# A decoder block with product-key experts: the gate of the one-hot masks moves from VectorE to ACT, and dot rows move from one stage to the next

## What is computed

```python
q = (h @ w_q).reshape(T, 8, 256)
s1 = einsum('thd,kd->thk', q[..., :128], k1)     # 128 keys each
s2 = einsum('thd,kd->thk', q[..., 128:], k2)
v1, i1 = top_k(s1, 16);  v2, i2 = top_k(s2, 16)
top, pos = top_k(all 256 sums of v1 and v2, 16)
idx = i1 * 128 + i2 at pos;  g = softmax(top)    # 8 heads x 16 experts a token
act = gelu(einsum('thkd,td->thk', u_tab[idx], h)) * g
out = einsum('thk,thkd->td', act, v_tab[idx])    # 16384 experts of width 2048
```

## Time and profile before

| | |
|---|---|
| median of 3 runs | 1833.39 us (1832.21 to 1834.75) |
| profiled execution | 1831.69 us |
| its span | 1829.7 us |
| TensorE busy | 1792.3 us, 98% |
| VectorE busy | 1586.5 us, 87% |
| ACT busy | 824.2 us, 45% |
| mean granted TensorE clock | 0.998 |
| HBM traffic | 337 GB/s over the span |

### The profile page before, as it was taken

One profiled execution on the slowest core, in us unless ns is written; L12 is line 12 of the kernel. 1 busy time (PEld: TensorE's weight loads), 2 busy tenths in 40 slices (PEclk: granted clock), 3 DMA queues, 4 the chain that ended last, 5 costly groups with the idle time before them and its releaser, 6 DMA issues.

```text
span 1829.7 us, 29108 instructions
## 1 busy us (share of the span) xinstructions
PE 1792.3 (98%) x9962; PEld 1571.9 (86%) x9962; DVE 1586.5 (87%) x2605; ACT 824.2 (45%) x1187; POOL 207.4 (11%) x193
## 2 busy tenths in 40 slices
PE   6999999999999999999999999999999999999998
PEld 6878888445999999999999999997888888888886
DVE  4668899966778999999999999998888888888887
ACT  3011222302635554333566666664555555555544
POOL 1000000110000000110122111121111111111110
PEclk9999999999999999999999999999999999999999
DMA  9998766798686667988899999999999999999994
GB/s 385 420 422 339 278 253 252 283 422 356 253 323 247 239 240 251 376 330 329 333 347 371 362 357 363 364 359 378 385 366 370 365 369 372 366 370 365 371 372 206
DMA packets 98193, 617.98 MB, mean 338 GB/s; under 512 B 13233, under 2 KB 21969, under 8 KB 26449
## 3 DMA queue, kind: packets, MB, share of 16 engines
q1 hardware_dynamic: 61456, 415.26, 59.0%
q0 software_dynamic: 25408, 184.58, 26.5%
q10 hardware_dynamic: 11266, 17.32, 2.5%
HBM read 600.26 MB, written 16.79 MB: 337 GB/s over the span
## 4 chain that ended last, share of the span: by engine, by line
PE 77%; DVE 10%; DMA 9%; issue 3%; ACT 1%; SPq 0%; DVEq 0%; ACTq 0%
PE ps L1320 30%; PE ps L960 15%; PE ps L967 9%; DMA raw<-in_w_ada 6%; PE ps L1005 6%; PE ps L1121 5%; PE ps L1175 4%; PE ps L1272 2%; PE ps L1016 2%; DVE big L1402 2%; DVE raw L1427 1%; DVE w_low L1380 1%; DMA big<-in_w_gate_f 1%; DVE big L1483 1%; DMA raw<-in_peer_v 1%
## 5 line engine op out<-in xcount | busy, mean ns | idle before, releaser
L673 ACT ACTIVATE w_hi<-raw 128x1024 fp32r<-128x1024 f32 x520 | 551.0, 1060 | 492.6 <-PE ps L1320 239.4
L1380 DVE TENSOR_TENSOR w_low<-raw,w_hi 128x1024 fp32r<-128x1024 f32 x520 | 632.9, 1223 | 89.6 <-ACT w_hi L673 82.8
L1320 PE MATMUL ps<-w_hi,a 128*128 128x512 f32 x1536 | 390.2, 389 | 0.5 <-issue 0.3
L960 PE MATMUL ps<-a,w_hi 128*128 128x384 f32 x1856 | 374.2, 343 | 0.9 <-issue 0.8
L1320 PEld LDWEIGHTS ps<-w_hi,a 128*128 128x128 f32 x1536 | 288.3, 188 | 60.9 <-ACT w_hi L673 0.5
L960 PEld LDWEIGHTS ps<-a,w_hi 128*128 128x128 f32 x1856 | 316.0, 189 | 1.9 <-issue 1.7
L1320 PE MATMUL ps<-w_low,a 128*128 128x512 f32 x1024 | 274.3, 390 | 1.2 <-DVE w_low L1380 1.2
L967 PEld LDWEIGHTS ps<-a,w_low 128*128 128x128 f32 x1856 | 238.1, 191 | 7.7 <-DVE w_low L1380 7.4
L967 PE MATMUL ps<-a,w_low 128*128 128x192 f32 x1856 | 241.3, 272 | 2.9 <-DVE w_low L1380 2.5
L1320 PEld LDWEIGHTS ps<-w_low,a 128*128 128x128 f32 x1024 | 191.9, 188 | 42.2 <-DVE w_low L1380 2.6
L1427 DVE CUSTOM_DVE_ANT_0 raw<-raw,big 128x2048 f32<-128x2048 f32 x64 | 146.2, 2290 | 67.0 <-DMA raw<-in_w_ada 64.3
(11 more groups left out here) (227 smaller groups left out, 1683.6 us busy)
## 6 DMA issues: line engine op xcount, KB each, us to landing
raw<-in_peer_u SPq DMA_DIRECT2D x128, 1024.0 KB, 6.0
raw<-in_peer_v SPq DMA_DIRECT2D x128, 1024.0 KB, 7.0
early<-in_w_front SPq DMA_DIRECT2D x56, 1024.0 KB, 9.1
raw<-in_w_ada POOLq DMA_DIRECT2D x48, 1024.0 KB, 8.2
raw<-in_w_ada SPq DMA_DIRECT2D x32, 1024.0 KB, 12.6
raw<-in_peer_wq SPq DMA_DIRECT2D x16, 1024.0 KB, 4.8
big<-in_w_gate_f SPq DMA_DIRECT2D x16, 1024.0 KB, 7.0
gel_saved<-stage ACTq DMA_DIRECT2D x64, 192.0 KB, 7.0
```

The lines of the kernel that those rows point to most:

```text
L673: act.activation(w_hi[:, h % 2, :], raw[:, s % RING, :], ACT.Copy).then_inc(hi_ready, 1)
L960: done = pe.matmul(ps[:, b % 2, 0:2 * TD].rearrange("p (m t) -> p m t", m=2), w_hi[:, ph.nth(j) % 2, k * P:(k + 1) * P], a_pair[:, kc, :, ...
L1320: done = pe.matmul(ps[:, 4 * tt + 2 * (j % 2) + n, :], a, w[:, n * 512:(n + 1) * 512], start=i is None and blk == 0 and m in (0, 2), stop= ...
L1380: dve.tensor_tensor(w_low[:, s % RING, :], raw[:, s % RING, :], w_hi[:, h % 2, :].bitcast(F32), ALU.subtract).then_inc(lo_ready, 1)
```

## The change

The gate leaves VectorE: one `tensor_tensor` compares both indices of four tokens (1024 columns), and ACT multiplies the second mask by the gate in four activations with a per-partition scale, in place, ahead of the put of the same unit. A new semaphore, oh_made, goes from VectorE to ACT, and ACT signals oh_ready to TensorE. ROUTE is written as 4 trips of 32 units with 12 groups each; MASK and USE are at the same units as before, two of the puts (the last of each 16 units) are a unit or two later except at a trip's end. Of the 64 rows for dots MID keeps 8 (16 half dots go), ROUTE has 56: the half dots of a steady trip of 32 units are behind every unit but 2, 10, 18 and 26. MID's plain units are 3 and 11 of each trip, 8 in all; the other 16 are split.

```diff
-PH_MID = Phase(PH_UP, EXPERT_BLOCKS // 32, 16, plain=(1, 3, 7, 9, 11, 15))
-PH_ROUTE = Phase(PH_MID, EXPERT_BLOCKS // 16, 16)
+PH_MID = Phase(PH_UP, EXPERT_BLOCKS // 32, 16, plain=(3, 11))
+PH_ROUTE = Phase(PH_MID, EXPERT_BLOCKS // 32, 32)
...
-USE_FIRST, MASK_FIRST, PUT_FIRST = (5, 7, 9, 11, 13, 15), (4, 6, 8, 10, 12, 14), (7, 9, 11, 13, 15, 15)
-USE, MASK, PUT = (1, 4, 6, 9, 12, 14), (0, 3, 5, 8, 11, 13), (3, 6, 8, 11, 14, 15)
-DOTS_MID_FIRST, DOTS_MID = tuple(range(8, 16)), (1, 2, 5, 6, 9, 10, 13, 14)
-DOTS_ROUTE_FIRST = DOTS_ROUTE = (0, 1, 3, 4, 5, 6, 8, 9, 11, 12, 13, 14)
+MASK_FIRST, MASK = (4, 6, 8, 10, 12, 14, 16, 19, 21, 24, 27, 29), (0, 3, 5, 8, 11, 13, 16, 19, 21, 24, 27, 29)
+USE_FIRST, USE = [tuple(j + 1 for j in at_units) for at_units in (MASK_FIRST, MASK)]
+PUT_FIRST, PUT = (7, 9, 11, 13, 15, 17, 19, 22, 24, 27, 30, 31), (3, 6, 8, 11, 14, 16, 19, 22, 24, 27, 30, 31)
+N_MASKS = len(MASK)
+DOTS_MID_FIRST, DOTS_MID = (11, 12, 14, 15), (3, 4, 11, 12)
+DOTS_ROUTE_FIRST = DOTS_ROUTE = tuple(j for j in range(32) if j % 8 != 2)
...
+            def gate_masks(g, i):
+
+                act.wait_ge(oh_made, at(i, N_MASKS, g + 1))
+                for t in range(4):
+                    token = bass.ds(at(i, 4 * N_MASKS, 4 * g + t), 1)
+                    done = act.activation(masks[:, 1, t, :], masks[:, 1, t, :], ACT.Copy, scale=sel_T[:, 2, token])
+                done.then_inc(oh_ready, 1)
+
+            def route(j, i, mask_at, put_at):
+
+                for g in range(N_MASKS):
+                    if mask_at[g] == j:
+                        gate_masks(g, i)
+                for g in range(N_MASKS):
                     if put_at[g] == j:
                         put_weights(g, i)
...
             def make_masks(g, i):
 
                 if i is not None or g:
-                    dve.wait_ge(oh_used, at(i, 6, g))
-                dve.tensor_tensor(masks[:, 0], iota[:, None, :].to_broadcast([P, 4, P]),
-                                  sel_T[:, 0, bass.ds(at(i, 24, 4 * g), 4)].unsqueeze(2).to_broadcast([P, 4, P]),
-                                  ALU.is_equal)
-                for t in range(4):
-                    token = bass.ds(at(i, 24, 4 * g + t), 1)
-                    done = dve.tensor_scalar(masks[:, 1, t, :], iota[:, :], sel_T[:, 1, token], sel_T[:, 2, token],
-                                             ALU.is_equal, ALU.mult)
-                done.then_inc(oh_ready, 1)
+                    dve.wait_ge(oh_used, at(i, N_MASKS, g))
+                tokens = sel_T[:, 0:2, bass.ds(at(i, 4 * N_MASKS, 4 * g), 4)]
+                dve.tensor_tensor(masks, iota[:, None, None, :].to_broadcast([P, 2, 4, P]),
+                                  tokens.unsqueeze(3).to_broadcast([P, 2, 4, P]), ALU.is_equal).then_inc(oh_made, 1)
```

More of the change, by code:

```diff
@@ L305, in build_block @@
                                                                  sem("selT_copied"))
-        oh_ready, oh_used, w_evac = sem("oh_ready"), sem("oh_used"), sem("w_evac")
+        oh_made, oh_ready, oh_used, w_evac = sem("oh_made"), sem("oh_ready"), sem("oh_used"), sem("w_evac")
         gel_out = (sem("gel_out0"), sem("gel_out1"))
@@ L786, in put_weights @@
             def put_weights(g, i):
-                act.wait_ge(oh_used, at(i, 6, g + 1))
-                act.activation(routed_by_token[:, bass.ds(at(i, 24, 4 * g), 4), :],
+                act.wait_ge(oh_used, at(i, N_MASKS, g + 1))
+                act.activation(routed_by_token[:, bass.ds(at(i, 4 * N_MASKS, 4 * g), 4), :],
                                ps[:, 2 + g % 6, :].rearrange("p (a b) -> p a b", a=4), ACT.Copy).then_inc(w_evac, 1)
-            def route(j, i, put_at):
-                for g in range(6):
+            def gate_masks(g, i):
[9 more added lines that the diff above has]
+                for g in range(N_MASKS):
                     if put_at[g] == j:
@@ L858, in _ @@
                     act.wait_ge(row_gate_in, 16 * SLICES)
-                route(j, None, PUT_FIRST)
+                route(j, None, MASK_FIRST, PUT_FIRST)
             with act.Fori(1, PH_ROUTE.n) as i:
@@ L862, in _ @@
                     up_unit(PH_ROUTE, j, i)
-                    route(j, i, PUT)
+                    route(j, i, MASK, PUT)
             def high_group(g, i, made):
@@ L1266, in weights @@
             def weights(g, i):
-                pe.wait_ge(oh_ready, at(i, 6, g + 1))
-                if i is not None:
-                    pe.wait_ge(w_evac, at(i, 6, g - 5))
+                pe.wait_ge(oh_ready, at(i, N_MASKS, g + 1))
+                if i is not None or g >= 6:
+                    pe.wait_ge(w_evac, at(i, N_MASKS, g - 5))
                 for t in range(4):
-                    done = pe.matmul(ps[:, 2 + g, t * P:(t + 1) * P], masks[:, 1, t, :], masks[:, 0, t, :], start=True,
+                    done = pe.matmul(ps[:, 2 + g % 6, t * P:(t + 1) * P], masks[:, 1, t, :], masks[:, 0, t, :], start=True,
                                      stop=True)
```

## The result

The changed kernel takes 1865.05 us (median of 6 runs, 1863.04 to 1870.10) against 1833.03 of the kernel before: the ratio is 1.0176, with a 95% interval of 1.0164 to 1.0189. That is 32.0 us more; the forecast was +27.2 and 1860.5, and its range of 1842 to 1884 holds the time. The profiled execution took 1863.04 us, its span is 1861.2 (before: 1829.7).

A forecast was written before the change was run, and what follows sets the result against it. ROUTE's steady part was taken as TensorE's, MID as VectorE's. With the change, 3 x (93.9 - 86.0) + 3.6 - 1.1 + 1.0 = +27.2 us, forecast as 1860.5 us, range 1842 to 1884.

The forecast's parts named there:

- (a): MID: 16 units become split and 16 half dots leave; VectorE keeps the pace, -1.1 us, ends -5.0 and +1.
- (b): ROUTE, VectorE alone: one-step comparison takes its list from 84.0 to 82.3 us, under TensorE's 86.0, changing nothing alone.
- (c): ROUTE: comparison, gate, put and hi through ACT take 4.56 us, making a steady trip 91.4 against TensorE's 86.0.
- (d): ROUTE's gathers: six half dots a steady trip wait 0.4 us each for rows, +2.5, making it 93.9.
- the gathers take over: Rival in ROUTE: landings stay at 7.7, VectorE waits 9.6 us a trip, +57 to 1890.7 us; 8% chance.
- (e): ROUTE's first trip of 32 units: 90.9 us, 92.9 with four short rows at 0.5, +3.6 over before.
- (f): Step into DOWN: VectorE's last half dot moves to the very last unit, delaying DOWN's first high copy, +1.0 us.
- (g): Loop turns: fewer of them fall beside work, claimed to change nothing.

The follow-up runs named there:

- e7: Kernel before with one-step comparison and the four gate activations on ACT, behind the next unit's hi; 12 rows per 32 units kept: 1831.48 us.
- e9: Changed kernel without the gate multiplication, and with the dot rows and plain units of the kernel before: 1831.77 us.
- e11: Changed kernel with gathers of half length for the dot rows, gate still ahead of the next unit's hi: 1854.78 us.
- e1: Changed kernel with ACT's gate moved behind the copy to w_hi of the next unit, nothing else: 1871.30 us.
- e3: Changed kernel without the gate multiplication, second mask left unweighted, 14 rows a trip: 1861.07 us.
- e6b: Changed kernel with gathers of half length and the gate as one activation of 512 columns in place of four of 128: 1836.40 us.
- e10: Changed kernel with the gate behind the next unit's hi and gathers of half length: 1842.72 us.
- e12: Changed kernel with the gate behind the next unit's hi and both half dots of a ROUTE row in one unit: 1846.60 us.
- e2: Changed kernel with masks compared and gated on VectorE again, rest of the change kept: 1873.37 us.
- e4: Kernel before with ROUTE written as 4 trips of 32 units and 12 groups, nothing else: 1834.64 us.
- e5: Kernel before with one-step comparison and the gate on ACT ahead of the next unit's hi; 12 rows per 32 units, trips of 16: 1836.82 us.

## Why the prediction was right, and where it wasn't

**(a) MID.** Forecast -1.1, measured 161.6 to 160.0, -1.6, with the weight loads' waits for w_low growing from 4.6 to 8.2 us. Another 1.6 us was gained ahead of MID's first subtraction (719.19, before 720.77). All eight profiled kernels with MID as changed reach the first mark at 886.8 to 888.8, and the five with MID as before at 889.6 to 890.7, so it isn't chance; where it comes from was not tried.

**(b) VectorE's list.** A comparison of 1024 columns occupies 1.14 from start to start (1092.73 to 1093.87), as taken. That the lighter list alone changes nothing is e7 and e9.

**(c) The loop.** Path 4.53 against 4.56. The four activations take 1.28 from first start to last end, above the end of 1.24 given for them, but the put starts 1.18 after the first, and that is what the path needs; 1.16 was taken. The estimate from the Trainium skill's "ScalarE: Activation LUTs", section What ACT_TABLE_LOAD costs, was 1.18 for four (worked out again, its figures give 1.17), and this row agrees with it. In the second trip VectorE waited 1.01 to 1.04 for w_hi in units 4, 9, 12, 20, 25 and 28, six of the seven that were named. In unit 17 it didn't: the half dot just ahead of it had waited 1.90 for its row, and w_hi was there by then, so one delay covered the other. e11, with hardly a wait for rows, has the loop's trip at 91.9 and 91.2 without the turns, and 91.4 was forecast. (The ends of that sum don't follow from the ends given for the gate: 1.04 and 1.24 make 90.0 and 92.4, not 89.8 and 92.3; nothing hangs on it.)

**(d) The rows.** This is the step whose number held and whose meaning didn't. Half dots waited 7.2 us in three trips, 2.4 a trip, where 2.5 was forecast. But I had worked out the rows' waits at the loop's pace only, as an addition of 2.5 to 91.4, and never asked what trip they allow by themselves. In e1 the four trips took 99.2, 95.4, 95.1 and 97.1 us, in e3 96.7, 96.9, 90.1 and 91.9 (the fourth up to DOWN's first subtraction), so 96.7 and 93.9 on average. In the changed kernel the loop's idle time on VectorE had hidden most of it: half dots waited 7.2 us in 975 to 1262 there and 31.2 in e1. Two limits of nearly the same height lie over one another, and removing either uncovers the other. The prediction had a rival called "the gathers take over", but with the loop in place beside it and at 1890; what the runs showed is a takeover at the forecast's own height. The reader would have been misled in what to mend: e1, the mending that the prediction's account suggests, gains nothing. So the steady trip came out right by the sum, and the cause that it names is only half of the account.

**(e) The first trip.** 95.6 against the 92.9 forecast. In 882 to 975 us half dots waited four times for rows, 4.7 us, where four waits of 0.5 had been put in: this term was 2.7 too small. In e11, with 2.1 us of such waits, the first trip took 93.2; without them it is 90.9 and 91.0 in the two kernels, and the sum had 90.9.

**(f) Into DOWN.** Behind ROUTE's last subtraction DOWN's first product came after 6.2 us, before after 5.0: +1.2, forecast +1.0.

**(g) "Fewer turns of the loop: nothing"** was wrong in sign. Between two trips ACT stands still. ACT's timeline in after at the first of two turns, then TensorE's:

```profile
1064.55 1.10 ACT L791 ACTIVATE big<-ps 128x512 f32 x1
1069.43 1.06 ACT L675 ACTIVATE w_hi<-raw 128x1024 fp32r<-128x1024 f32 x1 [3.78 <-issue]
```

```profile
1067.61 1.03 PE L980 MATMUL ps<-a,w_low 128*128 128x192 f32 x8
1070.84 2.64 PE L973 MATMUL ps<-a,w_hi 128*128 128x384 f32 x8 [2.19 <-ACT stage L776]
1073.28 1.67 PE L980 MATMUL ps<-a,w_low 128*128 128x192 f32 x8
```

"issue" means that ACT waited for nothing that the profile shows. From the subtraction of a trip's last unit to that of the next trip's first it is 5.80 us here and 6.07 at the next turn, against 3.85 where the first trip, which stands ahead of the loop, passes into it; that is 2.0 and 2.2 (in e6b, which has turns and no gap, it is 4.28 and 4.26, so some 0.4 of it comes with any turn), and without it these trips are 93.7 and 93.8, where 93.9 was forecast. So the sum: -1.1 became -3.2; the first trip +2.7 over its forecast; two turns +4.2; DOWN about as said. The total was 4.8 us short, all of it from rows in the first trip and from the turns, less what MID gave.

One wait was not foreseen at all: the weight load of the add of low waited 9.6 us, ten times, for ACT's copy of low. It is the same queue. Low stands behind gate and put too, and only hi had been followed.

## What to carry to other kernels

When a step is moved to an idle engine, look at what is queued behind it there and follow the path back to the first engine; the idle share (38% of ACT here) says nothing about it. Where the sum holds a second, smaller limit, work out what that limit would allow alone: a cycle of buffers is its landing time plus the time the consumer holds it, times the cycles in a trip. And an experiment that removes the named cause without getting the time back can be the sign of a second limit of the same height; vary both, as in the table, before undoing either.

## What the runs showed of the hardware that was not expected

**ACT's gap at a turn of its loop.** It appears in five kernels, all with trips of 32 units and four gate activations a group (after, e1, e10, e11, e12), at 3.8 to 4.8 us a turn. e2, e3, e4, e6b and e9 have trips of 32 units too, with fewer instructions on ACT, and no gap above 2.0; so have e5 and e7, with the gate but trips of 16. From the pages, one of the queues that load instructions, after and then e4:

```profile
q14 instruction: 40, 0.33, 0.0%
```

```profile
q14 instruction: 30, 0.25, 0.0%
```

It moved 40 packets in all five kernels with the gap and 25 to 30 in the nine without. The same queue in after, in 1050 to 1180 us only, which has both turns of the loop:

```profile
q14 instruction: 8, 0.07, 0.1%
```

In e11 it is 9, and in e4 and e6b none. e6b settles which engine it is: its kernel differs from e11's only in ACT's gate, one activation in place of four, and it has neither the gap nor these packets. So the gap goes with the length of ACT's loop. The Trainium skill, "Runtime: NRT & Kernel Launch", section Instruction fetch mechanics, says that instructions are loaded in blocks and that a taken branch whose target isn't in the window that is held forces a load before anything goes on. The gap and the packets agree with it: the longer loop no longer seems to be held whole. That ACT waits for these very packets is not shown, since the profile names no releaser.

**TensorE's clock behind a wait.** Windows of after around that turn, columns as above:

```profile
1060.00:1070.00 10.00, 8.52 (x62) 8.21 (x60) 8.37 (x12) 6.04 (x11) 2.83 (x2) 1.00 0.90 352
1070.00:1080.00 10.00, 9.16 (x54) 9.17 (x55) 8.47 (x10) 6.61 (x16) 1.68 (x1) 0.83 0.73 283
1080.00:1090.00 10.00, 9.96 (x74) 9.80 (x74) 8.49 (x11) 7.69 (x15) 1.68 (x1) 1.00 0.97 359
...
1071.00:1074.00 3.00, 3.00 (x12) 3.00 (x13) 3.00 (x5) 2.51 (x6) 0.00 (x0) 0.53 1.01 421
```

TensorE had been idle for 2.19 us; then the granted clock was 0.83 over ten us, and 0.53 in 1071 to 1074, which is nearly all at the lower of its two levels, 1.2 GHz and not 2.4. The hi part took 2.64 and not 1.66 as in the earlier trace rows. In e1, whose waits for rows reach TensorE, the same happened at 910 to 920 us (0.66) and elsewhere, and the mean of 887 to 1262 us is 0.97 against 0.99 in after. A late row so costs its wait and then some of the clock, which may be why e1 is above after; the two parts weren't separated. It isn't needed for the rows' limit, though: e1 was granted 1.00 from 1060 to 1155 us, and seven cycles of a buffer took 94.75 there.
